# A 512-column product for the first layer's input projections, with the norm factor multiplied in by GpSimd

## The reference

```python
u = _rmsnorm(h, norm_pre[i])
proj = u @ w_in
xb, gate = proj[..., :LRU_WIDTH], proj[..., LRU_WIDTH:]
xc = conv(xb, conv_w) + conv_b          # 4 taps along the tokens, per feature
r = sigmoid(blockwise(xc, w_r) + b_r)   # 8 blocks of 256 x 256
i = sigmoid(blockwise(xc, w_i) + b_i)
log_a = -8 * r * softplus(-lam)
a = exp(log_a);  bterm = sqrt(-expm1(2 * log_a)) * (i * xc)
h = scan(a, bterm)                      # along the tokens
y = (h * silu(gate)) @ w_out
```

## Time and profile before

| | |
|---|---|
| time, median of 3 runs | 2089.61 us (2087.47 to 2090.19) |
| profiled execution, its span | 2089.8 us (the page gives no other time for it) |
| instructions | 31175 |
| TensorE busy | 2052.2 us, 98% |
| VectorE, ScalarE, GpSimd busy | 75%, 50%, 4% |
| HBM read | 443.63 MB |

### The profile page before, as it was taken

One profiled execution on the slowest core, in us unless ns is written; L12 is line 12 of the kernel. 1 busy time (PEld: TensorE's weight loads), 2 busy tenths in 40 slices (PEclk: granted clock), 3 DMA queues, 4 the chain that ended last, 5 costly groups with the idle time before them and its releaser, 6 DMA issues.

```text
span 2089.8 us, 31175 instructions
## 1 busy us (share of the span) xinstructions
PE 2052.2 (98%) x12480; PEld 1804.9 (86%) x12480; DVE 1568.9 (75%) x2370; ACT 1035.9 (50%) x1560; POOL 81.4 (4%) x73
## 2 busy tenths in 40 slices
PE   8999999999999999999999999999999999999997
PEld 8999999888888888998888888788888888888886
DVE  6889986779798686678879898576766756656665
ACT  6876445656423223545555555555445435434543
POOL 0000020110000000000000001200000000000012
PEclk9999999999999999999999999999999999999999
DMA  7778897667524666444438989555875766555552
GB/s 289 233 245 288 299 319 261 235 197 256 162 99 158 206 236 228 140 143 131 141 131 311 336 289 343 164 173 193 275 239 190 258 215 197 181 190 195 188 178 98
DMA packets 122690, 449.87 MB, mean 215 GB/s; under 512 B 13745, under 2 KB 14129, under 8 KB 122033
## 3 DMA queue, kind: packets, MB, share of 16 engines
q1 hardware_dynamic: 122544, 447.88, 63.2%
HBM read 443.63 MB, written 4.19 MB: 214 GB/s over the span
## 4 chain that ended last, share of the span: by engine, by line
PE 72%; DVE 2%; ACT 1%; issue 0%; POOL 0%; POOLq 0%; ACTq 0%; DVEq 0%
PE bank L859 72%; DVE WL L1558 0%; DVE AR L1565 0%; PE bank L1017 0%; DVE SR L1565 0%; ACT WH L1157 0%; DVE AR L1558 0%; ACT AR L1157 0%; ACT AR L1158 0%; ACT L1158 0%; POOL AR L2165 0%; PE bank L1048 0%; ACT SR L1158 0%; POOL AR L2167 0%; DVE AR L1661 0%
## 5 line engine op out<-in xcount | busy, mean ns | idle before, releaser
L859 PE MATMUL bank<-SR,WH 128*128 128x512 f32 (+1 forms) x6240 | 1715.1, 361 | 15.9 <-DVE WL L1558 7.6
L859 PE MATMUL bank<-SR,WL 128*128 128x256 f32 (+1 forms) x4960 | 1124.7, 285 | 1.6 <-DVE SR L1565 1.6
L859 PEld LDWEIGHTS bank<-SR,WL 128*128 128x128 f32 x4960 | 936.8, 189 | 168.5 <-DVE SR L1565 3.0
L859 PEld LDWEIGHTS bank<-SR,WH 128*128 128x128 f32 x6240 | 986.5, 190 | 64.6 <-issue 18.4
L1157 ACT ACTIVATE WH<-WF 128x1024 fp32r<-128x1024 f32 x636 | 671.5, 1057 | 483.7 <-PE bank L859 431.0
L1558 DVE TENSOR_TENSOR WL<-WF,WH 128x1024 fp32r<-128x1024 f32 x636 | 770.2, 1223 | 127.0 <-ACT WH L1157 123.1
L1157 ACT ACTIVATE AR<-bank 128x256 f32<-128x256 f32 (+1 forms) x262 | 107.1, 413 | 312.8 <-PE bank L859 309.5
L1565 DVE SCALAR_TENSOR_TENSOR AR<-WF,SM,AR 128x512 f32<-128x512 f32 (+1 forms) x210 | 208.2, 1017 | 4.6 <-DMA WF<-in_mod 0.2
L1558 DVE TENSOR_TENSOR AR<-AR 128x256 f32<-128x256 f32 (+3 forms) x366 | 149.3, 438 | 48.7 <-ACT AR L1158 33.2
L1558 DVE TENSOR_TENSOR AR<-bank,AR 128x256 f32<-128x256 f32 (+1 forms) x234 | 100.3, 431 | 99.0 <-ACT AR L1157 68.9
L2160 POOL TENSOR_TENSOR AR<-AR 128x256 f32<-128x256 f32 x56 | 68.1, 1216 | 1990.8 <-ACT AR L1158 1990.7
(11 more groups left out here) (90 smaller groups left out, 546.6 us busy)
## 6 DMA issues: line engine op xcount, KB each, us to landing
WF<-in_mlp SPq DMA_DIRECT2D x256, 512.0 KB, 4.0
WF<-in_mod SPq DMA_DIRECT2D x192, 512.0 KB, 5.1
WF<-in_w_in SPq DMA_DIRECT2D x176, 512.0 KB, 4.3
WF<-in_a_in SPq DMA_DIRECT2D x64, 512.0 KB, 5.2
WF<-in_a_out SPq DMA_DIRECT2D x32, 512.0 KB, 6.1
WF<-in_ple_g SPq DMA_DIRECT2D x32, 512.0 KB, 4.6
WF<-in_w_out SPq DMA_DIRECT2D x32, 512.0 KB, 5.9
WF<-in_pw SPq DMA_DIRECT2D x16, 512.0 KB, 3.4
```

The lines of the kernel that those rows point to most:

```text
L859: return tensor.matmul(o, l, r, start=start, stop=stop, skip_group_check=True)
```

## The change

27 tiles, `xb` 4 to 15 and `gate` 0 to 14, take the form with two matmuls per `kt`. The four xb tiles made together and `gate` 15 stay as they were, written in `WHOLE`. For each of the 27:

- `evac` is now ScalarE's copy of the right half, into XB or GT.
- `after` n = 1 is VectorE's addition of the left half, which frees the bank.
- GpSimd then multiplies XB or GT by RX (`pool_program`; counts `xb_p`, `gate_p`).
- The rest of the chain moves back by two half tiles for all xb and gate tiles: n = 3, 4, 5, 6 in place of 1, 2, 3, 4.

XB has 6 buffers in place of 4, GT 5 + 4 in place of 3 + 3. Each group of `gates` tiles stands one tile later (after xb 6, 10, 14 and gate 2; before after xb 5, 9, 13 and gate 1).

```diff
-HALVES = ("pleg", "cv", "cg", "q", "hout", "gh", "wout", "mlp1", "mlp2", "pw", "gc")
-WHOLE = (("pleg", 15), ("wout", 15))
-AFTER = {"xb": 4, "gate": 4, ...
+HALVES = ("xb", "gate", "pleg", "cv", "cg", "q", "hout", "gh", "wout", "mlp1", "mlp2", "pw", "gc")
+WHOLE = (("xb", 0), ("xb", 1), ("xb", 2), ("xb", 3), ("gate", 15), ("pleg", 15), ("wout", 15))
+AFTER = {"xb": 6, "gate": 6, ...
@@ timetable
-    for j in range(2, 8):
-        for n in range(2):
-            add("xb", "a_in", 2 * j + n)
-            if j > 2 and n:
-                add_spread()
-        if j % 2 == 0:
-            add("gates", "a_gates", j // 2 - 1)
+    for j in range(4, 16):
+        add("xb", "a_in", j)
+        if j > 5 and j % 2:
+            add_spread()
+        if j % 4 == 2:
+            add("gates", "a_gates", j // 4 - 1)
     for j in range(16):
         add("gate", "a_in", 16 + j)
-        if j == 1:
+        if j == 2:
             add("gates", "a_gates", 3)
@@ ScalarE, evac
+            if kind == "xb" and what not in WHOLE:
+                w.wait_ge(x_sq, 2)
+                w.wait_ge(xc_v, j - 5)
+                act(XB[:, j % 6, :], cross(what), ACT.Copy).then_inc(half_a, 1)
+            elif kind == "gate" and what not in WHOLE:
+                w.wait_ge(x_sq, 2)
+                w.wait_ge(ys_lo, j - 4)
+                act(GT[:, j % 5, :], cross(what), ACT.Copy).then_inc(half_a, 1)
@@ ScalarE, after
-            if kind == "xb" and n == 1:
+            if kind == "xb" and n == 3:
                 w.wait_ge(s_par, 32)
-                w.wait_ge(*left((kind, j)))
+                w.wait_ge(*(left((kind, j)) if (kind, j) in WHOLE else (xb_p, j - 3)))
...
-            elif kind == "gate" and n == 1:
-                w.wait_ge(*left((kind, j)))
-                w.wait_ge(gz, j - 2)
+            elif kind == "gate" and n == 3:
+                w.wait_ge(*(left((kind, j)) if (kind, j) in WHOLE else (gate_p, j + 1)))
+                w.wait_ge(gz, j - 3)
@@ VectorE, evac: only for tiles in WHOLE; after
+            if kind in ("xb", "gate") and n == 1 and (kind, j) not in WHOLE:
+                s = XB[:, j % 6, :] if kind == "xb" else GT[:, j % 5, :]
+                w.wait_ge(half_a, COPIED[kind] + j + 1)
+                tt(s, psum((kind, j)), s, ALU.add).then_inc(left((kind, j))[0], 1)
@@ GpSimd, ahead of its sums of squares
+        w.wait_ge(x_rs, 1)
+        for j in range(4, 16):
+            w.wait_ge(*left(("xb", j)))
+            pool.tensor_tensor(XB[:, j % 6, :], XB[:, j % 6, :], RX, ALU.mult).then_inc(xb_p, 1)
+        for j in range(15):
+            w.wait_ge(*left(("gate", j)))
+            pool.tensor_tensor(GT[:, j % 5, :], GT[:, j % 5, :], RX, ALU.mult).then_inc(gate_p, 1)
```

More of the change, by code:

```diff
@@ L362, in linear @@
             begin()
-            if (kind, j) in WHOLE:
+            if (kind, j) in WHOLE and kind != "gate":
                 settle()
@@ L1222, in evac @@
             ps, leave = psum(what), left(what)[0]
-            if kind not in ("xb", "gate"):
+            if kind not in ("xb", "gate") or what not in WHOLE:
                 w.wait_ge(*full(what))
-            if kind == "gates":
+            if kind == "xb" and what not in WHOLE:
[6 more added lines that the diff above has]
+                act(GT[:, j % 5, :], cross(what), ACT.Copy).then_inc(half_a, 1)
+            elif kind == "gates":
                 g, b, ri, n = j
```

47 lines of the change are left out of this document (23 added, 24 removed).

## The result

The changed kernel takes **2104.99 us** in the median (2102.24 to 2105.47, 4 runs), against 2089.9 for the kernel before, 4 runs beside it. The ratio is 1.007, 95% interval 1.0058 to 1.0082: 0.7% slower, 15 us, where 2 us less was forecast and 2092.5 was the upper end of the range. Over the 25 to 27 runs of the kernel before that the experiments had beside them, its median was 2090.0 to 2090.6.

The account below looks back on a forecast made before the run. TensorE, busy 98% of the span, was taken as the bound, with VectorE nearly full beside it (91% in most gate tiles). Terms -5.3 + 1.7 - 0.7 + 0 + 2.1 = -2.2 us gave 2087.4 us, range 2084.0 to 2092.5.

Parts of the forecast that it names:

- The cheaper product: 27 tiles of 16 kt: 0.348 us per kt instead of 0.360, 432 x 0.0122, so 5.3 us less.
- GpSimd's multiplication at nothing: 27 GpSimd multiplications, taken at 1.2 us each with 5.6 us of time, costed at nothing on the path.
- Place 1: First gates group: fourth gates tile waits for VectorE to free the bank of xb 6, 1.7 us more.
- Place 2: Gates groups 1 and 2: old waits of 1.1 us each shrink, 0.7 us less; without VectorE's lead about 1 more.
- Place 3: Gates group 3: fourth tile's wait for VectorE stays 0.5 us, change 0; without the lead 1.8 us more.
- Place 4: End of the gate tiles: aout 0 and aout 1 wait for VectorE, 2.1 us more (1.5 to 2.5).
- the third pair: Another pair of multiplications at the end of the gate tiles, making ys_lo of gate 15 1.77 us later.
- the prediction's own signs of being wrong: TensorE waits at borders without a gates group, ScalarE's last tap waits for GpSimd, or first gates group and aout 0 wait-free.
- The clock: Rival, chance 0.09: clock falls after two of the new waits, 1.7 us each, giving 2090.8 us.
- GpSimd was one: Rival, chance 0.12: GpSimd holds up ScalarE some 0.6 us per tile in 12 xb tiles, 7.2 us, giving 2094.6.
- the slower rivals: Rivals above the forecast: GpSimd 2094.6 (0.12), clock 2090.8 (0.09), only the wide matmul's own gain 2090.5 (0.05).

Follow-up runs that it names:

- experiment 4: Changed kernel with the product of the 27 tiles as three 256-column matmuls, leaving out 27 products: 2107.0 us.
- experiment 5: experiment 1 with the xb and gate product written as before, three 256-column matmuls per step, nothing left out: 2094.75 us.
- experiment 2: Changed kernel without GpSimd's 27 multiplications, so those tiles stay without the norm factor: 2093.96 us.
- experiment 1: Changed kernel with VectorE adding the halves of xb 6, 10, 14 and gate 2 at once in evac: 2092.18 us.
- experiment 7: experiment 1 with gates 13 and 14 whole and the last three chains begun two steps on, two pairs of multiplications at the end: 2091.72 us.
- experiment 9: experiment 7 with the multiplications on VectorE at n = 2 instead of GpSimd: 2089.55 us.
- experiment 10: The change on the 12 xb tiles alone, added early and multiplied on VectorE, all gate tiles as in the kernel before: 2086.34 us.
- experiment 3: The kernel before with 27 GpSimd multiplications added on a scratch tile, for which nobody waits: 2094.37 us.

## Why the prediction was wrong

**The cheaper product: right as a price, half right as a gain.** 0.348 us per `kt` was there to the nanosecond. But experiments 4 and 5 give 2.0 and 2.6 us for it, not 5.3: where VectorE or ScalarE sets the end of a tile (the `gates` groups, gate 6, gate 8, aout 0), TensorE only waits longer. The forecast said that what TensorE saves can come back as a wait, and then looked for such waits at four places only.

**GpSimd's multiplication at nothing: the first step that failed.** It was costed by its effect on those who wait for it, ScalarE's step two half tiles later, and there it is free indeed: no wait for it shows on the path. It was not costed by its effect on VectorE. The forecast read WL's mean of 1.27 us as an upper bound for that effect. It set a mean duration against 1.14 from one start to the next; the duration of a WL alone is 1.22 in the earlier trace rows. And it is the wrong row: GpSimd waits while WL runs, and the instruction behind WL pays, 0.42 becoming 0.97. The rule that the prediction cited from the Trainium skill, "SBUF — State Buffer", section Who interferes with whom, is that a VectorE instruction with two SBUF inputs and a GpSimd one that reads SBUF exclude each other for their whole length. The trace agrees in direction with both its sides: 1.65 us for a GpSimd multiplication that comes behind a WL, 1.78 for a WL that comes behind a multiplication, and 0.55 us on VectorE's next one. The prediction used it only for how long GpSimd takes. That was 1.2 us in the forecast and 1.7 in fact. The term that stood at nothing was 0.4 us of VectorE apiece, 11.5 us over the stretch, and without the multiplications the changed kernel is 11.0 us faster (experiment 2).

**Place 1 (+1.7): right place, right cause, size too small.** The wait was 2.87 us. Of the working, the bank was to be free 15.0 us after the end of xb 4 (43.12), and it was at 59.69, 16.6 after. The taps began at 1.34 instead of 0.9 (+0.4), and two multiplications of GpSimd took 0.48 and 0.55 (+1.0); the rest of the list is right to 0.2 us. TensorE came for the bank 13.7 us after that end in place of 13.3, so the wait is 1.7 + 1.6 - 0.4 = 2.9 us. Then the clock fell, 1.6 us more.

**Place 2 (-0.7): the step that cost most.** "VectorE frees the fourth tile's bank in time if it keeps the lead it has." It kept none. The 1.98 us of idle time were not a lead that could be spent in the new order: they were time in which VectorE waited for TensorE to end a tile, part of the 17 us of the group row above. In the new order VectorE has an addition that depends on ScalarE and is put behind WLs that depend on ScalarE's WH, and its idle time is now waits for ScalarE (22 us), at other times than before. With the four additions early they are 10.5 us, so about half of them came with the late additions. The list that was worked out for group 0 item by item would have given the answer for group 1 too: from the end of xb 10, a WL, a subtraction, three taps, a WL and the addition are 1.14 + 0.34 + 1.43 + 1.14 + 0.34 = 4.4 us by the earlier trace rows, 4.9 with GpSimd's 0.55, against the 2.2 us of three `gates` tiles: 2.7 us of wait, and 2.50 was measured. The text named "about 1 us more" without the lead. It was 2.5 and 2.2 us in the two groups, and 1.7 at half clock behind each. The gain of 0.7 was figured from old waits of 1.1 us in each group; that is right for group 1, but group 2 had 0.7. The ScalarE side of the step can't be read in the changed kernel, where ScalarE catches up while TensorE waits. In experiment 1 it held: the fifth tile of group 1 waits 0.3 us, and 0.35 are lost at the group's end.

**Place 3 (0): the same mistake.** Without the lead, the text said, 1.8 more; it was 3.0 us of wait in place of 0.5.

**Place 4 (+2.1): right by its number, and in its cause for half.** aout 0's last `kt` and aout 1 wait, and the timelines of VectorE and PE of the changed kernel answer to the earlier trace rows:

```profile
257.00 0.41 DVE L1566 TENSOR_TENSOR AR<-bank,AR 128x256 f32<-128x256 f32 x1
...
262.92 2.35 DVE L1566 TENSOR_TENSOR WL<-WF,WH 128x1024 fp32r<-128x1024 f32 x2
```

```profile
263.05 0.50 PE L859 MATMUL bank<-SR,WH 128*128 128x256 f32 x2 [1.16 <-DVE SR L1566]
...
264.19 0.50 PE L859 MATMUL bank<-SR,WH 128*128 128x256 f32 x2 [0.52 <-DVE WL L1566]
```

From the evacuation of gate 15 to WL it is 5.92 us, where 4.14 + 1.77 was worked out from the period of one pair. The two tile halves grew by 1.77 and 0.6 us, 2.4 where 2.1 was forecast; the stretch as a whole has 1.8, since aout 2 lost 0.5 less than before. Taking the third pair away again (experiments 7 and 9) gives back 1.2 and 1.1 us, not 2.4; aout 1 waits as long without it.

**Gate 6 (not in the forecast): +3.5.** A ScalarE copy out of a bank stands in its order behind a step that waits for VectorE, a WH and more, and TensorE's transposes wait for it. Timeline of ScalarE in the changed kernel, then of PE:

```profile
186.48 1.06 ACT L1158 ACTIVATE AR<-AR 128x1024 f32<-128x1024 f32 x1 [1.50 <-DVE AR L1573]
187.44 0.36 ACT L1157 ACTIVATE AR<-bank 128x256 f32<-128x256 f32 x1
187.71 1.05 ACT L1157 ACTIVATE WH<-WF 128x1024 fp32r<-128x1024 f32 x1
188.65 0.59 ACT L1157 ACTIVATE AR<-bank 128x512 f32<-128x512 f32 x1
```

```profile
189.29 0.66 PE L1008 MATMUL bank<-CN,AR 128*128 128x128 f32 x4 [1.88 <-ACT AR L1157]
```

Two things there are from the change: VectorE late by what it had to catch up, and ScalarE's copy of gate 5 (187.44), which is one of the 27 new ones. The clock fell behind this wait as well. The wait is one of the prediction's own signs of being wrong, TensorE waiting at a tile border without a `gates` group. In experiment 10, where the gate tiles are as before, this half tile takes 3.31 us again.

**The rivals.** The clock was one, at 0.09 and 1.7 us apiece, "it needs the waits to be longer than I work out": they were, and it fell four times and not two. GpSimd was one, but with ScalarE as the sufferer, 0.6 us a tile in twelve tiles; the mechanism was VectorE. Each was right in kind and given as an alternative to the forecast, where in fact the late addition, GpSimd's share in it and the clock came together, one making the next larger. The range, which took the bounds of each place apart and left the slower rivals out, could not hold that.

## What to carry to other kernels

An engine's idle time before an instruction that waits for TensorE is not a lead. When the order changes, work out the whole list item by item at every place where a bank or buffer is handed on, not at the first alone; a release that another engine waits for belongs at the head of the list, as the four additions of experiment 1 show (13 us for no work at all). Work given to an idle GpSimd is not free where VectorE is full: its price is read on the VectorE instruction behind the one that it meets. And a saving on the busiest engine should be placed where the next busiest has room: with the additions early and VectorE multiplying, the change on all 27 tiles takes 2089.2 us (stretch 221.1), and on the 12 tiles where VectorE had idle time 2086.3 (217.6).

## What was not expected of the hardware

- A GpSimd multiplication of two 128 x 256 SBUF tiles took 1.58 to 1.66 us in 24 of 27 cases when it started inside a VectorE instruction with two SBUF inputs (WL, 1.22), and VectorE's next instruction took 0.97 in place of 0.42 us; two took 2.66 us; where it started first, it took 0.74 and WL was 0.56 us longer. Without the multiplications the means fell back to those of the kernel before (420 and 746 ns; before, 417 and 755). Inside a subtraction of 0.41 us (experiment 3) it took 0.85 us mostly, and the next instruction was again about 0.5 us longer.
- TensorE's clock stood at 0.50 of full speed for about 3.4 us behind waits of 2.87, 2.50 and 2.21 us at the fourth `gates` tile, and stayed at 1.00 behind the waits of 1.33 to 1.83 at the same places in experiment 2. It is not the wait's length alone: behind the fourth of the long waits, in group 3 (3.00 us), it stayed at 1.00, and behind the 1.88 us before gate 6 it fell to 0.51. In experiment 4 it fell behind 2.49, 1.77, 2.28 and 1.15 us. So the loss at a wait of 1 to 3 us is either nothing or 1.7 us, and what decides is open.
- One kernel's executions differ by 4 us and more with the granted clock: experiment 7's took 2092.40 us at a mean of 0.993 and 2087.74 at 0.996. In the profiles the places are 10 to 20, 36 to 44 and 1340 to 1380 us, where it stood between 0.66 and 1.00. That bounds what a median of a few runs can say here.
